# Layer norm statistics in two halves about a lower-half pivot, and the roots of three norms moved from GpSimd's power to ScalarE's Sqrt with VectorE's reciprocal, in a two-block transformer kernel

## The chip, the cores and the metric

The kernel runs on one core of one Trainium2 chip. The metric is device time in microseconds (us), the median of several executions. A core has five engines that matter here: TensorE (PE; its weight loads are PEld), VectorE (DVE), ScalarE (ACT), GpSimd (POOL) and SyncE (SP, which issues DMAs). They run their own instruction streams and wait for each other by semaphores.

## The reference, cut to what matters

256 tokens of width 1024 pass through two transformer blocks in float32. The first has a recurrent branch, sparse attention and a convolutional feed-forward part; its second norm is an RMS norm. The second has attention with a spatial gating unit and a gated feed-forward part; both of its sums are followed by a layer norm over all 1024 columns.

```python
def rms_norm(x, g):
    x32 = x.astype(jnp.float32)
    y = x32 * lax.rsqrt(jnp.mean(x32 * x32, axis=-1, keepdims=True) + EPS)
    return (y * g.astype(jnp.float32)).astype(x.dtype)
...
def layer_norm(x, g, b):
    xf = x.astype(jnp.float32)
    mu = jnp.mean(xf, axis=-1, keepdims=True)
    var = jnp.mean(jnp.square(xf - mu), axis=-1, keepdims=True)
    return ((xf - mu) * lax.rsqrt(var + LN_EPS) * g.astype(jnp.float32) + b.astype(jnp.float32)).astype(x.dtype)
...
        x = layer_norm(DEEPNORM_ALPHA * x + mix, ln1_g[l], ln1_b[l])
        ffn = swiglu_ffn(x, w_gate[l], w_up[l], w_down[l])
        x = layer_norm(DEEPNORM_ALPHA * x + ffn, ln2_g[l], ln2_b[l])
```

## The kernel before

The 256 tokens are two tiles of 128, one token per partition, called tile 0 and tile 1 (`t`). All weights come from HBM as one stream of chunks (`CHUNKS`), mostly 128x2048 float32. For each chunk ScalarE writes a rounded high part (`split`, L614, into `WH`), VectorE the remainder (L1033, into `WL`), and TensorE multiplies high by high, low by high and high by low. Activations are kept in the same two parts (`BHL`, `CHL`, `AH`, `AL`). The program of each engine is one loop over the chunks, written out by hand: what an engine does for chunk `c` stands in `side(c)`, in that order, and nothing is reordered later.

Three places hold the norms that the change touches. A norm needs whole rows, so it lies between two stages of matmuls:

- **The RMS norm before the feed-forward part of block one** (chunk kind "wo"). VectorE adds the residual (L1298), ScalarE squares each half of 512 columns with a running sum (L809), VectorE joins the two sums (L1303), GpSimd raises the result to the power -0.5 (L576), VectorE scales (L1310), TensorE transposes (L1754), ScalarE and VectorE write the high and low parts of the transposed tile (L918, L1443).
- **Layer norm one** (chunk kind "wo2", `layer_norm(0)`), between the second block's output projection and the gated feed-forward part.
- **Layer norm two** (`layer_norm(1)`), after the last matmul; its halves go to the output by DMA (L535). This is the end of the program.

In a layer norm VectorE forms the residual sum of a half (`residual_sum`, L1515) with the row's sum in `ysum`, then the negative mean (`mean`, L1541). Then two things run side by side: ScalarE squares all 1024 columns about the mean (`norm_squares`, L930), and VectorE forms (y + (-mean)) * gain (`gain`, L1526). GpSimd turns the sum of squares into 1/sqrt(var + eps) in two instructions (`power`, L554 and L555), and VectorE finishes each half with * yrs + bias (`finish`, L1535). In VectorE's program `residual_sum` of tile 1's first half stands ahead of `finish` of tile 0.

`link(...)` marks an instruction whose engine waits for its own result before it goes on. In row 85.37 us below, L554 is another use of `power`, for the keys of block one.

Of the kernel before, what the change touches and what calls it, by code (L numbers as in the profile page):

```python
# [27 lines left out]
P = 128  # L28
TOK = 256
NT = TOK // P  # L30
DM = 1024
# [204 lines left out]
def two_block_program(nc, A_w, A_x, A_cols, A_consts, A_g1, A_g2, A_og, A_gln, A_ln1, A_ln2, A_ws, A_out):  # L236
    ctx = ExitStack()
    with ctx:
# [30 lines left out]
        IDR = put("IDR", [P, P], F32R)  # L269
# [15 lines left out]
        def const(name):  # L285
# [5 lines left out]
        half = small("half", 64)  # L291
# [36 lines left out]
        yss = small("yss", 4)  # L328
        yrs = small("yrs", 4)
        tmp = small("tmp", 80)  # L330
# [98 lines left out]
        m_hi, m_lo, x1_ready, x1_sq, x1_ss, x1_rstd, xn2_ready, xt2_done, xt2_hi = (sem(n) for n in (  # L429
            "m_hi", "m_lo", "x1_ready", "x1_sq", "x1_ss", "x1_rstd", "xn2_ready", "xt2_done", "xt2_hi"))  # L430
# [10 lines left out]
        y_mean, y_sq, y_rstd, y_ln, xt4_done, xt4_hi, xt4_lo, up2_silu, up2_prod = (sem(n) for n in (  # L441
            "y_mean", "y_sq", "y_rstd", "y_ln", "xt4_done", "xt4_hi", "xt4_lo", "up2_silu", "up2_prod"))
        up2_hi, up2_lo, z_gain, masks_ready, wt_ready, rnn_in, xw_ready, gate_t_done, x_sq2 = (sem(n) for n in (
            "up2_hi", "up2_lo", "z_gain", "masks_ready", "wt_ready", "rnn_in", "xw_ready", "gate_t_done", "x_sq2"))
        half_copied, halves_summed = sem("half_copied"), sem("halves_summed")

# [93 lines left out]
        def _(eng):  # L540
# [57 lines left out]
        def _(eng):  # L598
# [123 lines left out]
            def side(c):  # L722
# [82 lines left out]
                if kind == "wo" and i % 2:  # L805
                    for t in range(NT):
                        n = i // 2
                        eng.wait_ge(x1_ready, NT * n + t + 1)
                        eng.activation(JK[:, 2 * n + t, :], X1[:, t, 512 * n:512 * n + 512], ACT.Square, scale=DM ** -0.5,  # L809
                                       accum_out=ss1[:, 2 * t + n:2 * t + n + 1]).then_inc(x1_sq, 1)  # L810
# [1622 lines left out]
```

## Time and profile before

| | |
|---|---|
| median of 3 executions | 824.15 us (824.13 to 825.29) |
| the profiled execution: its own time | 824.04 us |
| the profiled execution: span from first to last instruction | 822.3 us |
| mean granted TensorE clock | 0.993 |
| PE busy | 808.8 us (98%) |
| VectorE busy | 588.0 us (72%) |
| ScalarE busy | 481.3 us (59%) |
| GpSimd busy | 31.3 us (4%) |

How to read it: an engine that is busy for 98% of the span sets the time nearly everywhere, so a change on the other engines can only matter where TensorE waits or has already ended. Times in rows are us from the span's start, and "idle before <-" names what ended an engine's idle time.

### The profile page before, as it was taken

The page shows a single profiled execution, that of the slowest core. Times are in us where ns is not written, and L with a number is a line of the kernel's source. Part 1 is how long each engine was busy: PE and PEld are TensorE (multiplying, and loading weights), DVE is VectorE, ACT ScalarE, POOL GpSimd, SP SyncE. Part 2 cuts the span into 40 slices and gives each one's busy share as a digit, 9 for nine tenths or more (in the row PEclk, how much of TensorE's full clock was granted, in tenths as well). Part 3 has the DMA queues.
Part 4 walks back from the last instruction along what each step waited for, and adds up shares of the span by engine and source line. Part 5 has one row for each costly group of instructions (what it writes and reads, how often), then busy time and mean ns, then how long its engine had stood idle before and what let it go on. Part 6 is the DMA issues. An engine that isn't in the chain of part 4 may idle for free.

```text
span 822.3 us, 12246 instructions
## 1 busy us (share of the span) xinstructions
PE 808.8 (98%) x4997; PEld 706.5 (86%) x4997; DVE 588.0 (72%) x751; ACT 481.3 (59%) x730; POOL 31.3 (4%) x46
## 2 busy tenths in 40 slices
PE   9999998999999999999999999999999999999996
PEld 8889896888898998988888888888788988888885
DVE  5684686898975775788677877877877655654655
ACT  6463676878666444667566656546665645544551
POOL 1103000000000000000000000020110000000000
PEclk9999998999999999999999999999999999999998
DMA  8436441514234675255545555574344554565441
GB/s 327 157 123 268 151 168 50 169 55 164 100 121 173 221 272 206 103 188 194 200 185 199 166 204 200 211 271 158 132 179 151 205 205 168 191 209 200 157 151 51
DMA packets 22631, 144.00 MB, mean 175 GB/s; under 512 B 2608, under 2 KB 3120, under 8 KB 8240
## 3 DMA queue, kind: packets, MB, share of 16 engines
q1 hardware_dynamic: 20880, 137.92, 47.2%
q10 hardware_dynamic: 1696, 5.31, 1.8%
q8 instruction: 39, 0.64, 0.3%
q14 instruction: 16, 0.13, 0.0%
HBM read 142.17 MB, written 1.05 MB: 174 GB/s over the span
## 4 chain that ended last, share of the span: by engine, by line
PE 91%; DVE 3%; ACT 3%; issue 1%; DMA 1%; POOL 0%; DVEq 0%; POOLq 0%; SPq 0%; ACTq 0%
PE PS L1678 19%; PE PS L1682 10%; PE PS L1731 9%; PE PS L1732 9%; PE PS L1735 9%; PE PS L1665 7%; PE PS L1666 6%; PE PS L1670 6%; PE PS L1825 2%; PE PS L1694 2%; PE PS L1791 1%; PE PS L1802 1%; PE PS L1995 1%; PE PS L1702 1%; PE PS L2003 1%
## 5 line engine op out<-in xcount | busy, mean ns | idle before, releaser
L1033 DVE TENSOR_TENSOR WL<-RAW,WH 128x2048 fp32r<-128x2048 f32 (+2 forms) x128 | 285.1, 2228 | 45.9 <-ACT WH L614 45.9
L614 ACT ACTIVATE WH<-RAW 128x2048 fp32r<-128x2048 f32 (+2 forms) x128 | 238.7, 1867 | 67.7 <-PE PS L1735 26.5
L1453 DVE TENSOR_TENSOR HLS<-PS,HLS 128x512 f32<-128x512 f32 x46 | 31.7, 689 | 92.8 <-ACT HLS L938 92.8
L1678 PE MATMUL PS<-CHL,WH 128*128 128x512 f32 x352 | 87.9, 392 | 0.0
L1665 PE MATMUL PS<-BHL,WH 128*126 128x256 f32 (+2 forms) x344 | 85.7, 287 | 0.4 <-ACT TI L788 0.4
L1666 PE MATMUL PS<-BHL,WH 128*126 128x256 f32 (+2 forms) x344 | 83.6, 282 | 0.0
L938 ACT ACTIVATE HLS<-PS 128x512 f32<-128x512 f32 x46 | 27.4, 595 | 90.8 <-PE PS L1682 86.4
L1678 PE MATMUL PS<-BHL,WH 128*128 128x512 f32 x320 | 79.9, 392 | 0.0
L1678 PEld LDWEIGHTS PS<-CHL,WH 128*128 128x128 f32 x352 | 63.9, 189 | 11.8
L1732 PE MATMUL PS<-WH,AL 128*128 128x512 f32 x176 | 68.8, 391 | 0.0
L1665 PEld LDWEIGHTS PS<-BHL,WH 128*126 128x126 f32 (+2 forms) x344 | 64.3, 187 | 5.2 <-issue 4.3
L1731 PE MATMUL PS<-WH,AH 128*128 128x512 f32 x176 | 68.7, 390 | 0.0
L1678 PEld LDWEIGHTS PS<-BHL,WH 128*128 128x128 f32 x320 | 58.1, 189 | 10.7
L1666 PEld LDWEIGHTS PS<-BHL,WH 128*126 128x126 f32 (+2 forms) x344 | 64.4, 187 | 0.0
L1731 PE MATMUL PS<-WH,BHL 128*128 128x512 f32 x160 | 63.2, 395 | 0.0
L1732 PE MATMUL PS<-WH,BHL 128*128 128x512 f32 x160 | 62.4, 390 | 0.0
L1735 PE MATMUL PS<-WL,AH 128*128 128x512 f32 x176 | 54.4, 390 | 0.0
L1682 PEld LDWEIGHTS PS<-CHL,WL 128*128 128x128 f32 x352 | 48.0, 190 | 3.4
L1682 PE MATMUL PS<-CHL,WL 128*128 128x256 f32 x352 | 49.1, 282 | 0.0
L1670 PE MATMUL PS<-BHL,WL 128*126 128x256 f32 (+2 forms) x344 | 47.7, 281 | 0.0
L1682 PEld LDWEIGHTS PS<-BHL,WL 128*128 128x128 f32 x320 | 43.6, 190 | 3.1
L1464 DVE SCALAR_TENSOR_TENSOR CG<-HLS,CV,CG 128x255 f32<-128x255 f32 (+1 forms) x96 | 44.1, 480 | 1.7
(312 smaller groups left out, 1379.2 us busy)
## 6 DMA issues: line engine op xcount, KB each, us to landing
RAW<-in_w_stream SPq DMA_DIRECT2D x108, 1024.0 KB, 4.8
RAW<-in_w_stream SPq DMA_DIRECT2D x11, 1008.0 KB, 4.9
RAW<-in_w_stream SPq DMA_DIRECT2D x8, 704.0 KB, 4.5
WF<-in_w_stream SPq DMA_DIRECT2D x2, 1024.0 KB, 4.7
LN<-in_ln ACTq DMA_DIRECT2D x2, 1024.0 KB, 5.4
WF<-in_w_stream SPq DMA_DIRECT2D x4, 294.0 KB, 2.9
X<-in_x SPq DMA_DIRECT2D x2, 512.0 KB, 4.2
RAW<-in_w_stream SPq DMA_DIRECT2D x2, 512.0 KB, 7.3
```

The source lines that it names most:

```text
L614: eng.activation(WH[:, c % NSLOT, 0:CHUNKS[c][2]], raw(c), ACT.Copy).then_inc(w_hi, 1)
L1033: eng.tensor_tensor(WL[:, c % NSLOT, 0:CHUNKS[c][2]], raw(c), f32(WH[:, c % NSLOT, 0:CHUNKS[c][2]]), ALU.subtract).then_inc(w_lo, 1)
L1453: eng.tensor_tensor(HLS[:, n % 4, :, :], PS[:, bank:bank + 2, 0:TOK], HLS[:, n % 4, :, :], ALU.add)\
L1464: ins = eng.scalar_tensor_tensor(o, HLS[:, i % 4, v, 0:TOK - s], col("fw", (2 - s) * 2 * N_UP + f), o, ALU.mult, ALU.add)
L1665: eng.matmul(out, wh, H[0:parts, k, :], start=(k == 0), stop=False)
L1666: eng.matmul(out, wh, L[0:parts, k, :], start=False, stop=False)
L1670: last = eng.matmul(out, wl, H[0:parts, k, :], start=False, stop=(k == nk - 1))
L1678: eng.matmul(PS[:, bank, :], wh, HL[:, k, :, :].rearrange("p a t -> p (a t)"), start=(k == 0), stop=False)
L1682: last = eng.matmul(PS[:, bank, 0:TOK], wl, HL[:, k, 0, :], start=False, stop=(k == KD - 1))
L1731: eng.matmul(out, H[:, k, tile], wh, start=(start and n == 0), stop=False)
L1732: eng.matmul(out, L[:, k, tile], wh, start=False, stop=False)
L1735: last = eng.matmul(out, H[:, k, tile], WL[:, s, lo_:lo_ + cols], start=False, stop=(stop and n == len(ks) - 1))
```

## The change

It has five parts.

1. A layer norm's squares are no longer taken about the mean of 1024 columns but about a pivot, the mean of the tile's lower 512 columns (`ypiv`, one new VectorE instruction behind the first residual sum). ScalarE squares the lower half as soon as the pivot is there (`norm_first`) and the upper half when its residual sum is there (`norm_root`). With S0 and S1 the two halves' sums, the variance is (all squares about the pivot) / 1024 - ((S0 - S1) / 1024)^2. GpSimd works out `yadd`, which is the lower half's part of it plus eps minus the correction, in four linked instructions, in place of two before.
2. ScalarE takes the root: Sqrt(upper squares / 1024 + `yadd`), and VectorE a reciprocal (`root`), in place of GpSimd's power. The RMS norm of block one gets the same: its pair of sums is joined inside ScalarE's Sqrt, and GpSimd has no part in it.
3. In a layer norm, `gain` is cut into halves, and `finish` of tile 0 stands ahead of `residual_sum` of tile 1's first half. For tile 1 of layer norm one each half's finish follows its own gain.
4. `root_table()` runs a one-column Sqrt on ScalarE ahead of each place, which brings Sqrt's table in. The built program has four table loads more than before: three of these, and one for Gelu at the second chunk of block one's feed-forward part.
5. `IDR`, a rounded copy of the identity matrix that nothing read, goes, with TensorE's wait for it.

```diff
@@ gpsimd
-            for t in range(NT):
-                eng.wait_ge(x1_ss, t + 1)
-                eng.tensor_tensor(rs1[:, t:t + 1], ss1s[:, t:t + 1], half[:, 0:1], ALU.pow).then_inc(x1_rstd, 1)
...
-            for n in range(2):
-                for t in range(NT):
-                    eng.wait_ge(y_sq, NT * n + t + 1)
-                    j = NT * n + t
-                    power(yrs[:, j:j + 1], yss[:, j:j + 1], 1, DM, LN_EPS, y_rstd)
+            for j in range(2 * NT):
+                d, add, s = ydif[:, j:j + 1], yadd[:, j:j + 1], 2 * j
+                eng.wait_ge(y_first, j + 1)
+                link(eng.tensor_scalar(add, ysqa[:, j:j + 1], 1.0 / DM, LN_EPS, ALU.mult, ALU.add))
+                eng.wait_ge(y_half, j + 1)
+                link(eng.tensor_scalar(d, ysum[:, s:s + 1], ysum[:, s + 1:s + 2], 1.0 / DM, ALU.subtract, ALU.mult))
+                link(eng.tensor_tensor(d, d, d, ALU.mult))
+                eng.tensor_tensor(add, add, d, ALU.subtract).then_inc(y_add, 1)
@@ scalar
                         if i == 3:
+                            link(squares)
+                            eng.wait_ge(x1_ss, t + 1)
+                            eng.activation(std1[:, t:t + 1], ss1[:, 2 * t + 1:2 * t + 2], ACT.Sqrt,
+                                           bias=ss1s[:, t:t + 1]).then_inc(std_ready, 1)
...
-            def norm_squares(n, t):
+            def norm_first(n, t):
 
                 j = NT * n + t
-                eng.wait_ge(y_mean, j + 1)
-                eng.activation(YJ[:, t, :], (X1 if n == 0 else X3)[:, t, :], ACT.Square, bias=ymean[:, j:j + 1],
-                               accum_out=yss[:, j:j + 1]).then_inc(y_sq, 1)
+                eng.wait_ge(y_pivot, j + 1)
+                eng.activation(YJ[:, t, 0:512], (X1 if n == 0 else X3)[:, t, 0:512], ACT.Square, bias=ypiv[:, j:j + 1],
+                               accum_out=ysqa[:, j:j + 1]).then_inc(y_first, 1)
+
+            def norm_root(n, t):
+
+                j = NT * n + t
+                eng.wait_ge(y_half, j + 1)
+                link(eng.activation(YJ[:, t, 512:DM], (X1 if n == 0 else X3)[:, t, 512:DM], ACT.Square,
+                                    bias=ypiv[:, j:j + 1], accum_out=ysqb[:, j:j + 1]))
+                eng.wait_ge(y_add, j + 1)
+                eng.activation(ystd[:, j:j + 1], ysqb[:, j:j + 1], ACT.Sqrt, bias=yadd[:, j:j + 1], scale=1.0 / DM)\
+                   .then_inc(std_ready, 1)
+
+            def root_table():
+
+                eng.activation(junk[:, :], ident[:, 0:1], ACT.Sqrt)
@@ vector, residual_sum
-                link(eng.scalar_tensor_tensor(o, o, ALPHA, PS[:, 2 * t + h, :], ALU.mult, ALU.add,
-                                              accum_out=ysum[:, k:k + 1]))
+                ins = eng.scalar_tensor_tensor(o, o, ALPHA, PS[:, 2 * t + h, :], ALU.mult, ALU.add,
+                                               accum_out=ysum[:, k:k + 1])
+                if h:
+                    ins.then_inc(y_half, 1)
+                    eng.wait_ge(y_half, j + 1)
+                else:
+                    link(ins)
+                    eng.tensor_scalar(ypiv[:, j:j + 1], ysum[:, k:k + 1], -2.0 / DM, None, ALU.mult).then_inc(y_pivot, 1)
@@ vector, layer_norm
+                def root(t):
                     j = NT * n + t
-                    eng.wait_ge(y_rstd, j + 1)
-                    eng.wait_ge(y_gain, j + 1)
...
+                    eng.wait_ge(std_ready, NT + j + 1)
+                    link(eng.reciprocal(yrs[:, j:j + 1], ystd[:, j:j + 1]))
```

**Where instructions move.** VectorE at the end of the program, layer norm two, before (`X_158` is the tile being normed, `X_134` the gained copy):

```order
L1515 SCALAR_TENSOR_TENSOR X_158,ysum<-X_158,PS 128x512 x2
L1541 TENSOR_SCALAR ymean<-ysum 128x1
L1526 SCALAR_TENSOR_TENSOR X_134<-X_158,ymean,LN_159 128x1024
L1515 SCALAR_TENSOR_TENSOR X_158,ysum<-X_158,PS 128x512
L1535 SCALAR_TENSOR_TENSOR X_158<-X_134,yrs,LN_159 128x512
L1515 SCALAR_TENSOR_TENSOR X_158,ysum<-X_158,PS 128x512
L1541 TENSOR_SCALAR ymean<-ysum 128x1
L1526 SCALAR_TENSOR_TENSOR X_134<-X_158,ymean,LN_159 128x1024
L1535 SCALAR_TENSOR_TENSOR X_158<-X_134,yrs,LN_159 128x512 x3
```

and in the changed kernel, the same place, up to tile 1's mean (its gains, reciprocal and finishes follow as for tile 0):

```order
L1551 SCALAR_TENSOR_TENSOR X_164,ysum<-X_164,PS 128x512
L1558 TENSOR_SCALAR ypiv<-ysum 128x1
L1551 SCALAR_TENSOR_TENSOR X_164,ysum<-X_164,PS 128x512
L1586 TENSOR_SCALAR ymean<-ysum 128x1
L1568 SCALAR_TENSOR_TENSOR X_140<-X_164,ymean,LN_165 128x512 x2
L1574 RECIPROCAL yrs<-ystd 128x1
L1580 SCALAR_TENSOR_TENSOR X_164<-X_140,yrs,LN_165 128x512 x2
L1551 SCALAR_TENSOR_TENSOR X_164,ysum<-X_164,PS 128x512
L1558 TENSOR_SCALAR ypiv<-ysum 128x1
L1551 SCALAR_TENSOR_TENSOR X_164,ysum<-X_164,PS 128x512
```

Both of tile 0's finishes now precede tile 1's first residual sum; before, one stood between tile 1's two sums and the other behind tile 1's gain.

VectorE in layer norm one, tile 1, from the low parts of tile 0 (`BHL`) on, before:

```order
L1443 TENSOR_TENSOR BHL<-PS,BHL 128x2x128 x4
L1515 SCALAR_TENSOR_TENSOR X_134,ysum<-X_134,PS 128x512
L1541 TENSOR_SCALAR ymean<-ysum 128x1
L1526 SCALAR_TENSOR_TENSOR X_158<-X_134,ymean,LN_153 128x1024
L1535 SCALAR_TENSOR_TENSOR X_158<-X_158,yrs,LN_153 128x512 x2
```

and now, from the two instructions that have come in ahead of these low parts:

```order
L1551 SCALAR_TENSOR_TENSOR X_140,ysum<-X_140,PS 128x512
L1558 TENSOR_SCALAR ypiv<-ysum 128x1
L1478 TENSOR_TENSOR BHL<-PS,BHL 128x2x128 x4
L1551 SCALAR_TENSOR_TENSOR X_140,ysum<-X_140,PS 128x512
L1586 TENSOR_SCALAR ymean<-ysum 128x1
L1568 SCALAR_TENSOR_TENSOR X_164<-X_140,ymean,LN_159 128x512
L1574 RECIPROCAL yrs<-ystd 128x1
L1580 SCALAR_TENSOR_TENSOR X_164<-X_164,yrs,LN_159 128x512
L1568 SCALAR_TENSOR_TENSOR X_164<-X_140,ymean,LN_159 128x512
L1580 SCALAR_TENSOR_TENSOR X_164<-X_164,yrs,LN_159 128x512
```

The second half's gain has moved behind the first half's finish.

## Rows read from the trace of the kernel before

**Rows 1.** The page, part 4: the chain that ended last, by engine.

```profile
PE 91%; DVE 3%; ACT 3%; issue 1%; DMA 1%; POOL 0%; DVEq 0%; POOLq 0%; SPq 0%; ACTq 0%
```

**Rows 2.** TensorE's waits: total us, times, longest us.

```profile
PE PS L1754 <- DVE X L1535: 0.6, 1, 0.6
```

**Rows 3.** Timeline of VectorE, 806 to 823 us: start, duration, instruction, [idle before].

```profile
810.09 0.69 DVE L1515 SCALAR_TENSOR_TENSOR X<-X,PS 128x512 f32<-128x512 f32 x1
...
811.14 1.28 DVE L1526 SCALAR_TENSOR_TENSOR X<-X,ymean,LN 128x1024 f32<-128x1024 f32 x1
813.43 0.69 DVE L1515 SCALAR_TENSOR_TENSOR X<-X,PS 128x512 f32<-128x512 f32 x1 [1.00 <-PE PS L1735]
...
814.84 0.68 DVE L1515 SCALAR_TENSOR_TENSOR X<-X,PS 128x512 f32<-128x512 f32 x1
...
815.56 0.21 DVE L1541 TENSOR_SCALAR ymean<-ysum 128x1 f32<-128x1 f32 x1
815.81 1.28 DVE L1526 SCALAR_TENSOR_TENSOR X<-X,ymean,LN 128x1024 f32<-128x1024 f32 x1
817.01 0.75 DVE L1535 SCALAR_TENSOR_TENSOR X<-X,yrs,LN 128x512 f32<-128x512 f32 x1
818.47 1.42 DVE L1535 SCALAR_TENSOR_TENSOR X<-X,yrs,LN 128x512 f32<-128x512 f32 x2 [0.71 <-POOL yrs L555]
```

**Rows 4.** Timeline of ScalarE, 806 to 823 us.

```profile
815.81 1.15 ACT L930 ACTIVATE YJ<-X,ymean 128x1024 f32<-128x1024 f32 x1 [3.50 <-DVE ymean L1541]
```

**Rows 5.** Timeline of GpSimd, 806 to 823 us.

```profile
812.39 0.19 POOL L554 TENSOR_SCALAR tmp<-yss 128x1 f32<-128x1 f32 x1 [179.66 <-ACT YJ L930]
...
817.13 0.67 POOL L554 TENSOR_SCALAR tmp<-yss 128x1 f32<-128x1 f32 x1 [3.93 <-ACT YJ L930]
817.89 0.54 POOL L555 TENSOR_TENSOR yrs<-tmp,half 128x1 f32<-128x1 f32 x1
```

**Rows 6.** Timeline of GpSimd, two more instructions, elsewhere.

```profile
85.37 1.11 POOL L554 TENSOR_SCALAR tmp<-css 64x1 f32<-64x1 f32 x1 [11.14 <-ACT KSQ L665]
...
608.38 0.90 POOL L555 TENSOR_TENSOR ors<-tmp,half 128x1 f32<-128x1 f32 x1
```

**Rows 7.** Timeline of VectorE at these two times.

```profile
84.14 2.29 DVE L1033 TENSOR_TENSOR WL<-RAW,WH 128x2048 fp32r<-128x2048 f32 x1 [4.86 <-ACT WH L614]
...
608.12 0.75 DVE L1435 SCALAR_TENSOR_TENSOR MR<-MR,ors,OGR 128x512 f32<-128x512 f32 x1 [1.16 <-POOL ors L555]
```

**Rows 8.** Groups of instructions: count, busy us, mean ns, idle before.

```profile
L965 ACT ACT_TABLE_LOAD x1 | 1.3, 1283 | 0.0
L744 ACT ACTIVATE l<-l 126x11 f32<-126x11 f32 x1 | 0.2, 212 | 0.0
...
L1408 DVE RECIPROCAL ri<-rs 128x16 f32<-128x16 f32 x1 | 0.3, 254 | 0.1
...
L930 ACT ACTIVATE YJ<-X,ymean 128x1024 f32<-128x1024 f32 x4 | 4.6, 1153 | 17.8 <-DVE ymean L1541 17.8
```

**Rows 9.** Timeline of ScalarE at the RMS norm of block one.

```profile
318.14 0.63 ACT L809 ACTIVATE JK<-X 128x512 f32<-128x512 f32 x1 [2.96 <-DVE X L1298]
```

**Rows 10.** Timeline of VectorE, layer norm one.

```profile
624.02 1.29 DVE L1526 SCALAR_TENSOR_TENSOR X<-X,ymean,LN 128x1024 f32<-128x1024 f32 x1
...
626.33 1.42 DVE L1535 SCALAR_TENSOR_TENSOR X<-X,yrs,LN 128x512 f32<-128x512 f32 x2
628.28 1.42 DVE L1443 TENSOR_TENSOR BHL<-PS,BHL 128x256 fp32r<-128x256 f32 x4 [0.53 <-ACT BHL L918]
...
630.58 1.28 DVE L1526 SCALAR_TENSOR_TENSOR X<-X,ymean,LN 128x1024 f32<-128x1024 f32 x1
632.77 1.41 DVE L1535 SCALAR_TENSOR_TENSOR X<-X,yrs,LN 128x512 f32<-128x512 f32 x2 [0.90 <-POOL yrs L555]
```

**Rows 11.** Timeline of TensorE: tile 1's transposes at the two inner norms.

```profile
334.06 1.18 PE L1754 MATMUL PS<-CN,XN 128*128 128x128 f32 x8
...
633.57 1.32 PE L1754 MATMUL PS<-CN,X 128*128 128x128 f32 x8 [0.56 <-DVE X L1535]
```

More of the change, by code:

```diff
@@ L288, in two_block_program @@
         ident = const("ident")
-        half = small("half", 64)
+        half = small("half", 16)
         ssx = small("ssx", 4)
@@ L872, in side @@
                     evict_hi(CH, XT_BANKS["m"], mrt_done, mrt_hi, kps=(0, 1), first=2)
+                if kind == "wo2" and i == 0:
+                    root_table()
+                    norm_first(0, 0)
                 if kind == "wo2" and i == 2:
-                    norm_squares(0, 0)
+                    norm_root(0, 0)
                     split(c + 2)
@@ L997, in _ @@
                     eng.wait_ge(const_in, 32)
-                    eng.activation(IDR[:, :], ident, ACT.Copy).then_inc(masks_ready, 1)
                 if rg_group(c - W0, RG_INPUT) == NG - 1:
@@ L1521, in layer_norm, with gain, finish @@
                 gains, gains_in, landed = ((LN1, rows_in, 48), (LN2, rows_in, 64))[n]
[L1523 removed]
+                def gain(t, h):
                     j = NT * n + t
[L1525 to L1526 removed]
+                    half = slice(512 * h, 512 * h + 512)
+                    eng.scalar_tensor_tensor(gained[:, t, half], y[:, t, half], ymean[:, j:j + 1], gains[:, 0, half],
                                              ALU.add, ALU.mult).then_inc(y_gain, 1)
[L1529 removed]
+                def root(t):
                     j = NT * n + t
[L1531 to L1536 removed]
+                    eng.wait_ge(std_ready, NT + j + 1)
+                    link(eng.reciprocal(yrs[:, j:j + 1], ystd[:, j:j + 1]))
+                def finish(t, h):
+                    j = NT * n + t
+                    half = slice(512 * h, 512 * h + 512)
+                    eng.wait_ge(y_gain, 2 * j + h + 1)
+                    eng.scalar_tensor_tensor(X3[:, t, half], gained[:, t, half], yrs[:, j:j + 1], gains[:, 1, half],
+                                             ALU.mult, ALU.add).then_inc(y_ln, 1)
                 def mean(t):
@@ L1540, in mean @@
                     k = 4 * n + 2 * t
[L1541 to L1542 removed]
+                    link(eng.tensor_scalar(ymean[:, j:j + 1], ysum[:, k:k + 1], ysum[:, k + 1:k + 2], -1.0 / DM, ALU.add, ALU.mult))
                 if n == 0:
@@ L1547, in layer_norm @@
                     eng.wait_ge(gains_in, landed)
-                    gain(0)
+                    gain(0, 0)
+                    gain(0, 1)
+                    root(0)
+                    finish(0, 0)
+                    finish(0, 1)
                     residual_sum(0, 1, 0)
-                    finish(0)
                     tile_lo(BH, BL, XT_BANKS[4], xt4_hi, xt4_lo, 0)
@@ L1553, in layer_norm @@
                     mean(1)
-                    gain(1)
-                    finish(1)
+                    gain(1, 0)
+                    root(1)
+                    finish(1, 0)
+                    gain(1, 1)
+                    finish(1, 1)
                     tile_lo(BH, BL, XT1_BANKS[4], xt4_hi, xt4_lo, 1)
@@ L1561, in layer_norm @@
                     eng.wait_ge(gains_in, landed)
-                    gain(0)
+                    gain(0, 0)
+                    gain(0, 1)
+                    root(0)
+                    finish(0, 0)
+                    finish(0, 1)
                     residual_sum(1, 1, 0)
-                    finish(0, (0,))
                     residual_sum(1, 1, 1)
                     mean(1)
-                    gain(1)
-                    finish(0, (1,))
-                    finish(1)
+                    gain(1, 0)
+                    gain(1, 1)
+                    root(1)
+                    finish(1, 0)
+                    finish(1, 1)
             def gained_lo(kp):
```

70 lines of the change are left out of this document (38 added, 32 removed).

## The prediction

> **What bounds the kernel now.** I read the page's chain first: TensorE carries 91% of it [rows 1]. Then TensorE's waits, for the places where a norm holds it up. At the touched norms the only one of weight is 0.6 us, at layer norm one, where it waits for VectorE's finish [rows 2]. So the change can pay in two places: at layer norm one, up to that wait and what follows it, and behind the last matmul, where the norm's own chain is the time. The timelines of the tail show that chain: tile 1's last residual sum at 814.84, mean at 815.56, gain at 815.81 beside ScalarE's squares of 1.15 us, GpSimd's two instructions from 817.13 to 818.43, and two finishes from 818.47 to 819.89 [rows 3 to 5]. From there to the end of the span, 2.4 us, lies the last DMA, which the change leaves alone.
>
> **The tail, what is meant to go.** The long way from mean to finish is ScalarE 1.15 us, GpSimd 0.67, GpSimd 0.54, with hops. The squares of the lower half start earlier, and the power goes. But VectorE is then the engine with most to do: both finishes of tile 0 come ahead of tile 1's sums.
>
> **The tail, what comes in.** The four new GpSimd instructions fall beside VectorE's gains. The profile shows what happens there. GpSimd's one-column tensor_scalar takes 0.19 us when VectorE is quiet, but 0.67 when issued 0.12 us into a finish, and it ends at 817.80, just behind the finish's end at 817.01 + 0.75 = 817.76 [rows 3, 5]. The same form took 1.11 us at 85.37 and ended at 86.48, VectorE's L1033 beside it at 86.43; the power at 608.38 took 0.90 in place of 0.54 beside L1435 [rows 6, 7]. In all three VectorE reads two tensors from SBUF. The gain reads two as well. So I count a GpSimd instruction as held until VectorE's instruction ends, plus 0.05.
>
> The Trainium skill says this outright (SBUF — State Buffer, "Who interferes with whom"): a VectorE instruction with two SBUF inputs contends with a GpSimd instruction that reads SBUF, and the loser fully blocks, for the whole instruction. By that rule the tail gets slower, as in the sum below. The same page lets the first to start win; by that VectorE's gain would also wait for the first GpSimd instruction, at most its 0.19 us in each tile, which I leave out.
>
> Tile 0, step by step. The pivot takes the place of the second sum at 810.09. No row has this instruction; between nothing and the mean's 0.21 us [rows 3] I take 0.1, since only its issue holds VectorE. Second sum 810.19; from it to the gain were 1.05 us (810.09 to 811.14), so gain at 811.24. Two of 512 columns take 1.42 like the pair of finishes [rows 3]: to 812.66. ScalarE: pivot read at 810.3, then 0.63 us of squares of 512 columns [rows 9], and 0.17 to GpSimd's start as before (816.96 to 817.13) [rows 4, 5]: the first GpSimd instruction runs at 811.1 to 811.3, just ahead of the gain. The second is issued at 811.4 and held to 812.71. The third and fourth take 0.19 each with 0.09 between, as between 817.80 and 817.89 [rows 5]: 813.27. ScalarE's Sqrt costs 0.21, like the one small activation in the profile, and the reciprocal 0.25 [rows 8], with hops of 0.04 (818.43 to 818.47): finish at 813.85. For one column the reciprocal may be less, the Sqrt hardly; 0.1 us either way.
>
> Tile 1. Two finishes are passed in 1.34 (the pair's 1.42 less the second's overlap), so the first sum starts at 815.19. It stood at 813.43, before the finish. Pivot 0.72 later (814.84 to 815.56), second sum 816.01, mean 816.73, gains 816.98 to 818.40, second GpSimd instruction 818.45, fourth 819.01, Sqrt 819.26, reciprocal, finish 819.59. Before it was 818.47. **Tail: +1.1 us.** Without the hold the GpSimd chain would end before the gains: tile 0's finish 812.87, tile 1's sums 814.21 and 815.03, gains 816.0 to 817.34 (pitch), finish 817.63: -0.8 us. These are the bounds.
>
> **Layer norm one.** Tile 0's gain stays at 624.02. The third GpSimd instruction falls onto it and is held to 625.49; by the same steps the finish starts at 626.35, as before (626.33) [rows 10]. Then one sum and a pivot now follow these finishes where only a sum preceded them: VectorE was free at 627.75 (0.53 before 628.28), now it is at 628.5, and the low parts start 0.2 late. This passes on to tile 1's gain, 630.77. Only one half is gained: GpSimd is held to 631.57, fourth instruction 631.85, Sqrt 632.10, finish of the first half 632.43, against 632.77. But the second half's gain follows, and its finish waits for that gain: 633.90, against 632.77 + 0.67 = 633.44. TensorE transposes four blocks earlier and the last four 0.46 later than at 633.57 and on [rows 11]. Of this I take +0.3, since high and low parts of the four pieces ran in one row behind each other and hide some. Bounds: +0.5, and -0.2 without the hold, where both halves come 0.15 or more earlier. **+0.3 us.**
>
> **RMS norm of block one.** The power (0.54 us, as at 817.89 [rows 5]) and VectorE's join (one column, at most the mean's 0.21 [rows 3]) give way to Sqrt, 0.21, and reciprocal, 0.25 [rows 8], and one hop goes: 0.3 us less at most. But TensorE came to tile 1's transposes at 334.06 without idle before them [rows 11], so this is hidden. The cover is TensorE's own work on tile 0; without it the 0.3 would count. **0**, at best -0.1.
>
> **Four table loads** of 1.28 us [rows 8]. Ahead of the first squares of the RMS norm ScalarE idled 2.96 us [rows 9], and the four squares of the layer norms have 17.8 us of idle before them [rows 8], the first tile of each most of it: hidden. The one before Gelu follows ScalarE's copy, and TensorE has no wait in the feed-forward stage [rows 2]: hidden; bare it would cost 1.28. The dropped `IDR` frees ScalarE early, where nothing waits for it: 0.
>
> **Sum.** 822.3 + 1.1 + 0.3 = 823.7 us of span; the profiled execution lay 1.74 above its span and 0.11 under the median. **825.5 us.** A measurement of this kernel can tell about 0.2% (1.65 us) from no change, so this is no change that one can see.
>
> **Rivals.**
> - *GpSimd isn't held, or hardly* (one row of the same form, at 812.39, is clean; but VectorE had just gone quiet). -0.8 and -0.2 give 823.15. The new instructions would have to fall into gaps, and two gains stand back to back. 0.17.
> - *GpSimd slips in between the two gains.* No row shows a held instruction before a second VectorE instruction of that kind. One step of 0.28 less in each tile of the tail: 824.95. 0.17.
> - *The hold takes the first instruction too.* In the tail it is due 0.1 us from the gain in both tiles. If it misses, another 0.28 per tile in the tail, and 0.3 at layer norm one if its second is caught: 1.7 + 0.6 = +2.3 us, 826.4. This is the slower side: it decides once GpSimd's first instruction is issued after the gain. 0.14.
> - *A table load is bare* after all, for example at the end, if ScalarE's last high part comes late: at most 1.28 on top. 0.03.
> - *The forecast*: 0.49, its own range 825.0 to 826.0.
>
> The range of 823.1 to 826.1 leaves out most of the last two rivals. Faster by over 0.2% (under 822.5) needs more than the free case gives: 0.06. Slower (over 825.8) is the third rival, the fourth, and the upper edge of the forecast: 0.20. The rest, 0.74, is within 0.2%.
>
> **What would show it.** In the changed kernel's tail, GpSimd's second instruction in each tile should take over 1 us and end just behind the second gain; VectorE should idle 1.0 us or more before each reciprocal; the last finish should start near 819.6. At layer norm one the second half's transposes should wait about 0.5 us behind the first half's. I am wrong if GpSimd's four instructions take 0.19 each beside the gains, or if ScalarE's Sqrt takes much more than 0.21.

## The result, and the profile after

The changed kernel took 826.36 us (median of 17 executions, 823.95 to 828.42) beside 824.13 for the kernel before (17, 821.77 to 825.44). The ratio is 1.0029, with a 95% interval of 1.0020 to 1.0037: slower, by 2.2 us. The forecast was 825.5, with a range of 823.1 to 826.1; the time lies 0.26 above that range.

The page of the changed kernel, its head and part 1:

```profile
span 823.5 us, 12293 instructions
PE 807.4 (98%) x4997; PEld 705.9 (86%) x4997; DVE 590.2 (72%) x765; ACT 490.1 (60%) x750; POOL 32.9 (4%) x52
```

Where the 2.2 us are can't be read from two spans alone. The span grew by 1.2 in the profiled executions (822.3 to 823.5), but by 1.9 in the medians over all executions (822.2 to 824.1). And the time around the span, execution time less span, grew as well: 1.75 to 2.22 in the median.

The 0.7 us by which the profiled executions differ less is TensorE's clock, in a stage that the change doesn't touch. Here are four windows of the kernel before, columns as on the page's windows (length, busy time of each engine, PEclk, DMA share, GB/s):

```profile
130.00:132.00 2.00, 0.31 (x1) 0.31 (x2) 1.93 (x5) 1.36 (x3) 0.00 (x0) 0.90 0.87 359
132.00:134.00 2.00, 2.00 (x6) 1.08 (x7) 1.00 (x2) 0.00 (x0) 0.00 (x0) 0.50 0.24 101
134.00:136.00 2.00, 2.00 (x10) 0.84 (x7) 0.00 (x0) 0.34 (x1) 0.00 (x0) 0.50 0.00 0
136.00:138.00 2.00, 2.00 (x10) 1.26 (x11) 0.00 (x0) 2.00 (x5) 0.00 (x0) 0.50 0.00 0
```

and two of the same windows in the changed kernel:

```profile
134.00:136.00 2.00, 2.00 (x12) 0.92 (x8) 0.00 (x0) 0.51 (x2) 0.00 (x0) 0.71 0.00 0
136.00:138.00 2.00, 2.00 (x17) 1.17 (x16) 0.00 (x0) 2.00 (x4) 0.00 (x0) 1.00 0.00 0
```

Behind a stretch in which TensorE was nearly idle (busy 0.31 us of the first window's 2), its granted clock was 0.5, that is 1.2 GHz instead of 2.4, for 6.8 us in one execution and 3.4 in the other; in roots_only below not at all. Laid instruction by instruction against the kernel before, TensorE in the changed kernel comes out of this stage 1.51 us early and gives 0.77 back by 175 us, 0.43 of it in one wait for ScalarE at 161.8. What is left, 0.74, is luck of the execution, and has to be taken off before the rest is read. In such a comparison TensorE then falls behind at just two places: by 0.66 at 366.8 us and by 0.29 at 633.6; another 0.08 comes in small pieces between 586 and 629. Behind TensorE's work, the tail is longer by 0.88. Together 1.9, as in the median spans.

**The tail.** VectorE's timeline of the changed kernel, answering to [rows 3]:

```profile
809.65 0.69 DVE L1551 SCALAR_TENSOR_TENSOR X<-X,PS 128x512 f32<-128x512 f32 x1 [4.18 <-PE PS L2158]
...
811.42 1.44 DVE L1568 SCALAR_TENSOR_TENSOR X<-X,ymean,LN 128x512 f32<-128x512 f32 x2
813.61 0.17 DVE L1574 RECIPROCAL yrs<-ystd 128x1 f32<-128x1 f32 x1 [0.74 <-ACT ystd L961]
813.81 1.42 DVE L1580 SCALAR_TENSOR_TENSOR X<-X,yrs,LN 128x512 f32<-128x512 f32 x2
...
816.91 1.42 DVE L1568 SCALAR_TENSOR_TENSOR X<-X,ymean,LN 128x512 f32<-128x512 f32 x2
819.44 0.16 DVE L1574 RECIPROCAL yrs<-ystd 128x1 f32<-128x1 f32 x1 [1.12 <-ACT ystd L961]
819.64 1.42 DVE L1580 SCALAR_TENSOR_TENSOR X<-X,yrs,LN 128x512 f32<-128x512 f32 x2
```

From the first residual sum to the last pair of finishes it is 819.64 - 809.65 = 9.99 us; before it was 9.11, from the sum at 809.36, one 0.73 ahead of the first of [rows 3], to 818.47. GpSimd in the same stretch, answering to [rows 5]:

```profile
811.47 0.19 POOL L597 TENSOR_SCALAR yadd<-ysqa 128x1 f32<-128x1 f32 x1 [179.82 <-ACT YJ L951]
811.76 0.60 POOL L599 TENSOR_SCALAR ydif<-ysum 128x1 f32<-128x1 f32 x1
812.44 0.48 POOL L600 TENSOR_TENSOR ydif<-ydif 128x1 f32<-128x1 f32 x1
813.00 0.19 POOL L601 TENSOR_TENSOR yadd<-yadd,ydif 128x1 f32<-128x1 f32 x1
816.96 0.75 POOL L597 TENSOR_SCALAR yadd<-ysqa 128x1 f32<-128x1 f32 x1 [3.77 <-ACT YJ L951]
817.80 0.67 POOL L599 TENSOR_SCALAR ydif<-ysum 128x1 f32<-128x1 f32 x1
818.56 0.19 POOL L600 TENSOR_TENSOR ydif<-ydif 128x1 f32<-128x1 f32 x1
818.83 0.19 POOL L601 TENSOR_TENSOR yadd<-yadd,ydif 128x1 f32<-128x1 f32 x1
```

Where VectorE is quiet, three of the four take 0.19 each and the second 0.29 (gain_waits, below). In each tile two are held, and each ends 0.05 to 0.16 behind the end of one of the two gains: one goes through per gain, not one per pair. In tile 0 the second and third are held, and VectorE waits 0.74 for the root. In tile 1 it is the first and second, and it waits 1.12. The first is issued 0.05 us behind the start of the gain in both tiles, gets in in one and is held in the other; no run shows what decides that.

ScalarE, answering to [rows 4]: squares of 512 columns about a pivot, and a root:

```profile
810.57 0.72 ACT L951 ACTIVATE YJ<-X,ypiv 128x512 f32<-128x512 f32 x1 [6.01 <-DVE ypiv L1558]
...
819.11 0.29 ACT L961 ACTIVATE ystd<-ysqb,yadd 128x1 f32<-128x1 f32 x1 [1.54 <-POOL yadd L601]
```

**TensorE's waits**, two rows of that view of the changed kernel. The first answers to [rows 2], the second is new:

```profile
PE PS L1809 <- DVE X L1580: 0.8, 1, 0.8
PE PS L1790 <- DVE WL L1067: 0.6, 1, 0.6
```

**Gelu's table load.** ScalarE's, VectorE's and TensorE's timelines of the changed kernel, a row or two each. The load goes ahead of the first Gelu:

```profile
343.80 1.28 ACT L988 ACT_TABLE_LOAD   x1
345.10 0.42 ACT L988 ACTIVATE CG<-CG 128x256 f32<-128x256 f32 x1
```

```profile
345.55 0.42 DVE L1506 TENSOR_TENSOR CG<-CG 128x256 f32<-128x256 f32 x1 [0.55 <-ACT CG L988]
```

```profile
366.76 0.73 PE L1790 MATMUL PS<-WL,AH 128*128 128x512 f32 x2 [0.63 <-DVE WL L1067]
```

VectorE waits 0.55 for the Gelu. 21 us and four chunks later TensorE waits 0.63 for a low part of the weights. In between, VectorE's rows repeat every 5.87 us (346.80, 352.67, 358.54 for the low part of a chunk) and hold no idle time but the 0.48 that each chunk has before L1511, so it can't catch up; TensorE needs 5.59 per chunk (its own rows repeat at 348.27, 353.86 and 359.45) and runs up to it.

**Layer norm one**, tile 1, answering to [rows 10, 11]; VectorE, then TensorE's transposes:

```profile
632.07 0.16 DVE L1574 RECIPROCAL yrs<-ystd 128x1 f32<-128x1 f32 x1 [0.74 <-ACT ystd L961]
632.27 0.75 DVE L1580 SCALAR_TENSOR_TENSOR X<-X,yrs,LN 128x512 f32<-128x512 f32 x1
632.93 0.75 DVE L1568 SCALAR_TENSOR_TENSOR X<-X,ymean,LN 128x512 f32<-128x512 f32 x1
633.72 0.75 DVE L1580 SCALAR_TENSOR_TENSOR X<-X,yrs,LN 128x512 f32<-128x512 f32 x1
```

```profile
633.07 0.66 PE L1809 MATMUL PS<-CN,X 128*128 128x128 f32 x4
634.52 0.66 PE L1809 MATMUL PS<-CN,X 128*128 128x128 f32 x4 [0.79 <-DVE X L1580]
...
635.89 1.31 PE L1749 MATMUL PS<-BHL,WH 128*128 128x256 f32 x8 [0.21 <-DVE BHL L1478]
```

The first half of the transposes comes 0.5 early and the second waits 0.79 behind it. TensorE then waits 0.21 more for low parts, and has lost 0.29 by the end of the norm.

### The profile page after: what moved, and what is told of

It reads as the page before. It is cut to its first block, busy times and chain, and to the rows that moved or that the text cites. A ratio compares the mean times of both kernels' runs of the same rounds, so it can differ in the third digit from the quotient of the medians.

```text
span 823.5 us, 12293 instructions
## 1 busy us (share of the span) xinstructions
PE 807.4 (98%) x4997; PEld 705.9 (86%) x4997; DVE 590.2 (72%) x765; ACT 490.1 (60%) x750; POOL 32.9 (4%) x52
## 4 chain that ended last, share of the span: by engine, by line
PE 63%; issue 24%; DVE 6%; ACT 5%; DMA 1%; POOL 1%; DVEq 0%; SPq 0%; POOLq 0%; ACTq 0%
PE PS L1733 8%; PE PS L1790 7%; PE PS L1786 7%; PE PS L1787 7%; PE PS L1720 6%; PE PS L1721 6%; PE PS L1725 6%; PE PS L1737 4%; DVE WL L1067 2%; PE PS L1879 1%; PE PS L2049 1%; PE PS L1856 1%; PE PS L1845 1%; PE PS L1749 1%; ACT SM L642 1%
```

## The experiments

Eleven kernels, each compared with the kernel before on its own chip. "Around" is the median of execution time less span; "tail" runs from the first residual sum of layer norm two to its last pair of finishes in the profiled execution.

| kernel | median us (n) | before | ratio, 95% interval | around | tail |
|---|---|---|---|---|---|
| before | 823.98 (35) | | | 1.75 | 9.11 |
| changed | 826.36 (17) | 824.13 | 1.0029 (1.0020 to 1.0037) | 2.22 | 9.99 |
| gelu_early | 825.39 (12) | 823.98 | 1.0017 (1.0007 to 1.0027) | 2.24 | 9.64 |
| rms_power | 825.28 (11) | 823.98 | 1.0016 (1.0007 to 1.0024) | 1.74 | 9.99 |
| add_vector | 824.84 (12) | 823.98 | 1.0014 (1.0005 to 1.0023) | 1.75 | 9.04 |
| roots_only | 822.92 (12) | 823.98 | 0.9989 (0.9979 to 0.9999) | 1.72 | 8.70 |
| pool_probe | 824.13 (10) | 824.00 | 1.0001 (0.9990 to 1.0012) | 1.73 | 9.11 |
| load_only | 824.67 (11) | 824.00 | 1.0010 (0.9998 to 1.0021) | 1.73 | 9.11 |
| roots_order | 823.09 (11) | 824.00 | 0.9991 (0.9982 to 1.0000) | 1.78 | 8.34 |
| gain_waits | 826.86 (5) | 824.00 | 1.0037 (1.0024 to 1.0050) | 2.23 | 10.50 |
| pool_two_more | 825.36 (10) | 823.97 | 1.0014 (1.0003 to 1.0025) | 1.72 | 9.64 |
| vector_two_more | 825.63 (10) | 823.97 | 1.0020 (1.0012 to 1.0029) | 2.23 | 9.97 |
| roots_all | 823.12 (12) | 823.97 | 0.9983 (0.9973 to 0.9992) | 1.75 | 8.71 |

**gelu_early.** The changed kernel, with Gelu's table fetched behind the RMS norm's last root instead of at the first Gelu.

```diff
                             eng.activation(std1[:, t:t + 1], ...).then_inc(std_ready, 1)
+                            if t == NT - 1:
+                                eng.activation(junk[:, :], ident[:, 0:1], ACT.Gelu_apprx_tanh)
```

> The changed kernel with one more instruction: a one-column Gelu on ScalarE behind the Sqrt of tile 1 of the RMS norm, so that Gelu's table comes in at about 332 us, in an idle stretch of 1.9 us. Theory (the load in the feed-forward stage is bare, because ScalarE and VectorE together need 5.87 us per chunk there against TensorE's 5.59 and can't make up for it): TensorE's wait of 0.63 us for VectorE's low part at 366.8 goes, VectorE's idle of 0.55 before L1506 at 345.5 too, and the time falls by 0.6 us, from about 826.4 to 825.8. Rival (that wait has to do with TensorE having come early by the clock's shorter low stretch, not with the load): the wait stays and the time stays at 826.4.

The wait for `WL` was gone, and no offset of TensorE arose in the feed-forward stage. ScalarE loaded the table at 331.04 us, in idle time. The median was 1.0 us below the changed kernel's, with 0.6 expected: 0.65 for the load, and 0.35 because in its tail the first GpSimd instruction slipped in ahead of the hold in both tiles (VectorE waited 0.74 twice) and not in one. The time around the span stayed at 2.24.

**load_only.** The other side of it: the kernel before, with one Sqrt ahead of the RMS norm's squares and nothing else. It brings in two loads, Sqrt's there and Gelu's at 344 us.

```diff
                 if kind == "wo" and i % 2:
+                    if i == 1:
+                        eng.activation(junk[:, :], ident[:, 0:1], ACT.Sqrt)
```

> The kernel before plus the dummy Sqrt ahead of the RMS norm alone: two table loads more (Sqrt's in idle time, Gelu's in the feed-forward stage), nothing else. Theory: TensorE waits 0.6 us for a low part of the weights at about 367 us, and the time rises by 0.6 us to about 824.7. Rival (the wait needs something else of the change): no wait, 824.1.

Its view of TensorE's waits has the row again:

```profile
PE PS L1738 <- DVE WL L1036: 0.6, 1, 0.6
```

TensorE fell back by 0.65 at that place and nowhere else. The median rose by 0.67; its interval alone just reaches to no change, and the trace decides. vector_two_more, below, shows why medians alone would not do.

**rms_power.** The changed kernel with the RMS norm as it was: GpSimd's power, no Sqrt and so no load for it nor for Gelu.

```diff
+                eng.wait_ge(x1_ss, t + 1)
+                eng.tensor_tensor(rs1[:, t:t + 1], ss1s[:, t:t + 1], half[:, 0:1], ALU.pow).then_inc(std_ready, 1)
...
-                            eng.activation(std1[:, t:t + 1], ss1[:, 2 * t + 1:2 * t + 2], ACT.Sqrt,
-                                           bias=ss1s[:, t:t + 1]).then_inc(std_ready, 1)
```

> The changed kernel with block one's RMS norm as before (VectorE's join, GpSimd's power, no table load for Sqrt there and none for Gelu after it). Theory: everything that this part costs is the load before Gelu, so the time falls by 0.6 us to about 825.8, as with the early Gelu. Rival (the part's 0.3 us shorter norm pays in TensorE's stream): it falls by 0.3 or less, 826.1.

No wait in the feed-forward stage, as in gelu_early. The root itself is worth nothing there in either form. The median fell by 1.1 and not by the 0.6 expected: the time around the span was 1.74, a surprise, and that is the other 0.5. At layer norm one TensorE fell back by 0.59 in the profiled execution, twice as much as in the changed kernel, because ScalarE's Sqrt of tile 1 started 0.37 us behind GpSimd's last instruction and not 0.09; why it did is open. The tail was as long as the changed kernel's, with the tiles' parts exchanged: here it was tile 0 whose first GpSimd instruction was held:

```profile
811.16 0.75 POOL L600 TENSOR_SCALAR yadd<-ysqa 128x1 f32<-128x1 f32 x1 [180.10 <-ACT YJ L947]
...
816.99 0.19 POOL L600 TENSOR_SCALAR yadd<-ysqa 128x1 f32<-128x1 f32 x1 [3.76 <-ACT YJ L947]
```

**add_vector.** The changed kernel with `yadd` worked out on VectorE, in four one-column instructions more, and none on GpSimd.

```diff
+                    eng.tensor_scalar(ydif[:, j:j + 1], ysum[:, k:k + 1], ysum[:, k + 1:k + 2], 1.0 / DM, ALU.subtract, ALU.mult)
+                    eng.tensor_scalar(ydig[:, j:j + 1], ysum[:, k:k + 1], ysum[:, k + 1:k + 2], -1.0 / DM, ALU.subtract, ALU.mult)
...
+                    link(eng.tensor_scalar(ydif[:, j:j + 1], ydif[:, j:j + 1], ydig[:, j:j + 1], LN_EPS, ALU.mult, ALU.add))
+                    eng.wait_ge(y_first, j + 1)
+                    eng.scalar_tensor_tensor(yadd[:, j:j + 1], ysqa[:, j:j + 1], 1.0 / DM, ydif[:, j:j + 1], ALU.mult, ALU.add)\
+                       .then_inc(y_add, 1)
```

> The changed kernel with GpSimd's four one-column instructions gone; VectorE does the same arithmetic in four small instructions around the mean. Theory (GpSimd is held behind VectorE's gains): VectorE gets some 0.5 us more work per tile, but goes from gain to reciprocal without idle; tail's last finish 1.0 us earlier against its first sum than in the changed kernel (9.0 in place of 10.0 us), layer norm one 0.3 us earlier, time down by 1.3 us to about 825.1. Rival (the tail is long because VectorE has both finishes of tile 0 ahead of tile 1's sums): 0.5 us more work on VectorE per tile makes it longer, 0.5 to 1 us slower, about 827.

VectorE's timeline of this kernel, tile 1 of the tail:

```profile
817.77 1.41 DVE L1561 SCALAR_TENSOR_TENSOR X<-X,ymean,LN 128x512 f32<-128x512 f32 x2
819.10 0.16 DVE L1567 RECIPROCAL yrs<-ystd 128x1 f32<-128x1 f32 x1
819.29 1.41 DVE L1573 SCALAR_TENSOR_TENSOR X<-X,yrs,LN 128x512 f32<-128x512 f32 x2
```

No wait before the reciprocal. The tail is 9.04: the four instructions more delay each tile's gains by 0.57 us, and the whole is still 0.95 shorter than with GpSimd. At layer norm one TensorE falls back by 0.03 in place of 0.29. This shows that GpSimd's being late is what the changed tail pays for. It also shows that the two halves hardly gain anything even then: the tail is 0.07 below that of the kernel before, with VectorE busy nearly throughout it.

**gain_waits.** The hold tested by itself: VectorE's gains wait until GpSimd has finished, so nothing lies beside its four instructions.

```diff
+                    eng.wait_ge(y_add, j + 1)
```

> The changed kernel, in which VectorE's gains also wait until GpSimd's four instructions are through, so that none of them meets a gain. Theory (hold): GpSimd's take 0.19 each with 0.09 between, 0.9 us from the half's sum to the gain; the two gains then hide the Sqrt, and sum to finish takes 2.4 us per tile in place of 2.7 to 3.0: the tail gets 0.5 us shorter although VectorE is made to idle, time 825.9. At layer norm one, with one gain to hide behind, about nothing. Rival (no hold, GpSimd slow by itself): every instruction keeps its 0.5 to 0.7, the wait comes on top, and the tail gets 0.6 us longer per tile, 827.5.

GpSimd and VectorE in tile 1 of the tail of this kernel:

```profile
816.65 0.19 POOL L597 TENSOR_SCALAR yadd<-ysqa 128x1 f32<-128x1 f32 x1 [4.81 <-ACT YJ L951]
816.93 0.29 POOL L599 TENSOR_SCALAR ydif<-ysum 128x1 f32<-128x1 f32 x1
817.31 0.19 POOL L600 TENSOR_TENSOR ydif<-ydif 128x1 f32<-128x1 f32 x1
817.58 0.19 POOL L601 TENSOR_TENSOR yadd<-yadd,ydif 128x1 f32<-128x1 f32 x1
```

```profile
817.88 1.42 DVE L1569 SCALAR_TENSOR_TENSOR X<-X,ymean,LN 128x512 f32<-128x512 f32 x2 [1.32 <-POOL yadd L601]
```

The durations are those of a quiet VectorE: an instruction that was held for 0.48 to 0.75 us takes 0.19 when the gain is away, and the second, held for 0.60 to 0.67, takes 0.29. That decides for the hold. The time doesn't: the median of five executions lies 0.9 above the theory's and 0.6 below the rival's, and it went up, not down. From mean to finish it is 819.40 - 816.35 = 3.05 us, with 2.4 reckoned. The chain of four begins 0.30 us behind the start of the mean, since ScalarE's squares take 0.72, and costs 1.12; only then do the gains begin.

**pool_probe.** The hold measured on its own. The kernel before, with 60 pairs of a one-column tensor_scalar and a one-column memset on GpSimd, which nobody waits for, in the feed-forward stage of block one.

```diff
+            for _ in range(60):
+                link(eng.tensor_scalar(probe[:, 0:1], probe[:, 0:1], 1.0, 0.0, ALU.mult, ALU.add))
+                link(eng.memset(probe[:, 1:2], 0.0))
```

> The kernel before, with 120 extra GpSimd instructions on a scratch tile of its own, each linked to the one before: 60 times a one-column tensor_scalar (reads and writes SBUF) and a one-column memset (only writes), from about 333 us on, beside VectorE's work of the feed-forward stage. Theory (a GpSimd instruction that reads SBUF is held by a VectorE instruction with two SBUF inputs until that one ends, and slips in before the next): tensor_scalars take 0.19 us when VectorE is idle or reads PSUM (L1453), and up to 2.3 us beside L1033, ending 0.05 behind its end; beside the row of four L1464 they end one at each instruction's end, not behind the fourth. Memsets take about 0.1 to 0.2 everywhere. VectorE's own durations stay as they are (2.28, 0.48 each). Rival (first come, the whole engine held): tensor_scalars that have started hold VectorE, whose durations grow by up to 0.19. Time as before, 824.1. For the time outside the span: the program gets longer than the changed kernel's; if that time hangs on the program's total size, it rises from 1.75 to 2.2 us, otherwise it stays at 1.75.

GpSimd's timeline of this kernel, then VectorE's:

```profile
340.15 0.19 POOL L581 TENSOR_SCALAR probe<-probe 128x1 f32<-128x1 f32 x1
340.40 0.10 POOL L582 MEMSET probe<- 128x1 f32 x1
340.58 1.96 POOL L581 TENSOR_SCALAR probe<-probe 128x1 f32<-128x1 f32 x1
...
343.69 0.28 POOL L581 TENSOR_SCALAR probe<-probe 128x1 f32<-128x1 f32 x1
```

```profile
340.21 2.28 DVE L1039 TENSOR_TENSOR WL<-RAW,WH 128x2048 fp32r<-128x2048 f32 x1
342.40 1.91 DVE L1470 SCALAR_TENSOR_TENSOR CG<-HLS,CV,CG 128x255 f32<-128x255 f32 x4
```

Beside the one long instruction the tensor_scalar takes 1.96 us and ends at 342.54, 0.05 behind the 342.49 of VectorE. Beside the row of four short ones it takes 0.19 to 0.28: where one is held, it ends 0.05 behind the VectorE instruction that it started beside (the last one shown at 343.97, the third of the four at 343.92). The memset took 0.10 throughout. VectorE's durations stayed as they were (2283 ns for L1039, 480 for L1470), and the time did not change.

The Trainium skill (SBUF — State Buffer, "Who interferes with whom") says that a VectorE instruction with two SBUF inputs contends with a GpSimd instruction that reads SBUF, and that whoever issues first blocks the other for its whole instruction. For GpSimd as the second the trace agrees: 1.96 in place of 0.19 us. What the runs add is that the hold is one instruction long and not a row of them. For VectorE as the second the trace doesn't agree: GpSimd's tensor_scalar of 340.15 was under way when L1039 began at 340.21, and L1039 took 2.28 as in the kernel before.

**roots_only.** The kernel before with part 2 of the change for the layer norms alone: squares about the mean as they were, then ScalarE's Sqrt and VectorE's reciprocal; order, gain and RMS norm unchanged.

```diff
@@ scalar, norm_squares
+                eng.wait_ge(y_sq, j + 1)
+                eng.activation(ystd[:, j:j + 1], yss[:, j:j + 1], ACT.Sqrt, bias=lneps[:, 0:1], scale=1.0 / DM)\
+                   .then_inc(y_rstd, 1)
@@ vector, finish
-                    eng.wait_ge(y_rstd, j + 1)
+                    if 0 in halves:
+                        eng.wait_ge(y_rstd, j + 1)
+                        link(eng.reciprocal(yrs[:, j:j + 1], ystd[:, j:j + 1]))
```

> The kernel before with one part of the change alone: in the two layer norms ScalarE's Sqrt and VectorE's reciprocal in place of GpSimd's two instructions; squares about the mean, order of VectorE and RMS norm as before, Sqrt's table loaded ahead of the two places. Theory: the tail loses GpSimd's 0.67 + 0.54 and hops and gains 0.29 + 0.2, so the last finish starts at 817.9 in place of 818.5; layer norm one saves 0.2; time 0.6 to 0.8 us under before, 823.4. Rival (Sqrt with its load costs as much as the power): 824.1, no difference. If the time outside the span, which went from 1.74 to about 2.2 us with the change, hangs on the table loads or on Sqrt, it shows here too: then 823.9.

This one is faster than both kernels, than the one before by 0.11% (0.01 to 0.21). At layer norm one TensorE comes to tile 0's transposes 0.18 late, but its wait of [rows 2] is gone, and it comes out of the norm 0.37 earlier; the tail is 0.41 shorter. That is 0.8 us in the trace, the upper end of what was expected, and 1.1 in the medians. VectorE, tile 1 of the tail of this kernel:

```profile
813.48 1.28 DVE L1535 SCALAR_TENSOR_TENSOR X<-X,ymean,LN 128x1024 f32<-128x1024 f32 x1
814.68 0.74 DVE L1546 SCALAR_TENSOR_TENSOR X<-X,yrs,LN 128x512 f32<-128x512 f32 x1
815.35 0.15 DVE L1542 RECIPROCAL yrs<-ystd 128x1 f32<-128x1 f32 x1
815.53 1.41 DVE L1546 SCALAR_TENSOR_TENSOR X<-X,yrs,LN 128x512 f32<-128x512 f32 x2
```

There is no wait left before the reciprocal: the late half of tile 0's finish at 814.68 is what the root now waits for.

**roots_order.** roots_only with tile 0's finish in one piece ahead of tile 1's sums, as in the changed kernel.

```diff
+                    finish(0)
...
-                    finish(0, (0,))
...
-                    finish(0, (1,))
```

> The kernel with roots by ScalarE alone (squares about the mean), now with part three's order in layer norm two: both finishes of tile 0 ahead of tile 1's sums. Theory (with the root ready early, the order fills VectorE's idle second and takes a finish out of tile 1's chain): last finish 0.3 us earlier against the tail's first sum, 7.7 in place of 8.0 us; time 0.3 under roots alone, 822.6. Rival (the order as such is what makes the changed kernel's tail long, since tile 1's first sum comes 0.8 later): 0.5 us slower than roots alone, 823.4.

In the trace the tail is 8.34, 0.36 shorter than roots_only's: tile 1's gain starts 6.54 us behind the first sum in place of 6.65, and its finish 1.80 behind the gain in place of 2.05. The rest of the program is alike. So with the root ready early the order is no cost, and rather a gain; in the changed kernel it was not tested by itself. The medians don't show it (823.09 and 822.92, each with an interval of about 0.8 us either way), and which of the two is faster stays open.

**roots_all.** roots_only with the RMS norm's root on ScalarE as well, and the early load of Gelu's table.

```diff
+                            link(squares)
+                            eng.wait_ge(x1_ss, t + 1)
+                            eng.activation(std1[:, t:t + 1], ss1[:, 2 * t + 1:2 * t + 2], ACT.Sqrt,
+                                           bias=ss1s[:, t:t + 1]).then_inc(x1_rstd, 1)
+                            if t == NT - 1:
+                                eng.activation(junk[:, :], ident[:, 0:1], ACT.Gelu_apprx_tanh)
```

> Roots alone, as in roots_only, for both layer norms, with the RMS norm's root by ScalarE and VectorE's reciprocal too, and the Gelu table fetched early. Theory (the RMS norm's root is hidden behind TensorE's work on tile 0): no difference to roots_only, 822.9 us beside a kernel before at 824.0. Rival (some of it is on the path): 0.3 less, 822.6. If its time outside the span is 2.2 and not 1.7, the median is 0.5 higher, 823.4.

823.12, tail 8.71, and TensorE passes the RMS norm without an offset: the root there is hidden.

**pool_two_more and vector_two_more.** By then the time around the span was 2.2 in three kernels (changed, gelu_early, gain_waits) and 1.7 to 1.8 in all others, one with 120 more instructions among them. The three have the same numbers of GpSimd and VectorE instructions (52 and 765 on their pages). Both kernels here are the changed kernel with two memsets more at the start, of four columns each, one kernel on GpSimd and one on VectorE:

```diff
@@ gpsimd (pool_two_more)
+            link(eng.memset(ydif[:, :], 0.0))
+            link(eng.memset(yadd[:, :], 0.0))
@@ vector (vector_two_more)
+            link(eng.memset(ymean[:, :], 0.0))
+            link(eng.memset(yrs[:, :], 0.0))
```

> The changed kernel with two more one-column GpSimd memsets at the start of the program, where GpSimd is idle; nothing reads them. The time outside the span was 1.7 to 1.8 us in the kernel before and in five variants, and 2.2 in the changed kernel and in the two others that have the same numbers of GpSimd and VectorE instructions. Theory (the 0.48 us hang on how many instructions stand in an engine's program, or on where its last ones come to lie): with two more on GpSimd, time outside the span falls to 1.75 and the median to 825.9. Rival (they hang on something else that the changed kernel does): it stays at 2.2, and the median at 826.4.

> The changed kernel with two more one-column VectorE memsets at the start of the program; nothing reads what they write before it is written anew. Theory (number or place of instructions in VectorE's program): time outside the span falls to 1.75, median 825.9. Rival (GpSimd's program, or something else): it stays at 2.2, and the median at 826.4. If both kernels fall, the place of the whole program counts and not that of one engine; if neither does, the cause stays open.

With two more on GpSimd it fell to 1.72; with two more on VectorE it stayed at 2.23. Both kernels execute more than the changed one, so it isn't the work. It goes with GpSimd's program: 52 instructions on the page gave 2.2 in four kernels, and 36, 37, 39, 46, 54 and 167 gave 1.7 to 1.8 in the others. Of the rest of pool_two_more's 1.0 us, 0.35 is again the tail, where the first GpSimd instruction got in ahead in both tiles.

vector_two_more is also a warning. Its tail and its time around the span are those of the changed kernel, and yet its median, 825.63, is 0.73 below (826.4 was expected). Its executions had a higher mean clock more often: 0.996 or more in four of ten, against two of seventeen. That fits a difference of 0.7 us that the clock alone makes, and so the prices given here rest on the traces.

## Why the prediction was wrong

By its own steps, against the changed kernel:

- **"Four table loads … the one before Gelu follows ScalarE's copy, and TensorE has no wait in the feed-forward stage: hidden."** This is the step that failed. It cost 0.65 us (TensorE's loss at 366.8 us in the changed kernel and in load_only): the wait for `WL` appears in these two and in the others with the load at the Gelu, and not in gelu_early, rms_power or roots_all. That TensorE didn't wait in that stage said only that VectorE was no later than it. The view to read was VectorE's rhythm: no idle time in a chunk but the one after each Gelu, on a path that runs through ScalarE, so whatever delays the Gelu stays in the row. The price lay between the forecast's 0 and its bare 1.28. The rival that named it had 0.03.
- **"The profiled execution lay 1.74 above its span", taken as unchanged.** It became 2.22, 0.48 more. Two GpSimd memsets take it away again, so it comes with how GpSimd's program happens to lie or to be counted. No row shows it. What of the program sets it stays open.
- **The tail, +1.1.** Measured +0.88. GpSimd is held by the gains, as forecast (gain_waits, pool_probe, add_vector). Two sizes were off. The hold lasts one VectorE instruction, so one of GpSimd's slips in between the two gains, which was the rival of 824.95. That takes off what the rival said, 0.28 per tile: with neither first instruction caught the tail is +0.53 (gelu_early, pool_two_more), where 1.1 less 0.56 was the rival's figure. And the first instruction is sometimes caught too, the rival of 826.4, in one tile of two here; that adds 0.35 (+0.87 to +0.88 with one caught). The two partly cancel, and the forecast came out near by luck, for a reason it did not name. The rival's condition was wrong as well: the first instruction was issued behind the gain's start in all ten tiles of the five kernels with this code, and in seven of them it got in. ScalarE's root took 0.29 where 0.21 was reckoned, its squares 0.72 where 0.63, and the reciprocal 0.16 where 0.25.
- **The signs that the prediction named** came out in part: GpSimd's second instruction took 0.60 and 0.67 and not over 1 us, VectorE idled 0.74 and 1.12 before the reciprocals, and the last finish started at 819.64 as forecast, but from a first sum 0.29 later. And one of the prediction's rows doesn't bear its rule of "plus 0.05": the power at 608.38 ended at 609.28, 0.41 behind L1435's end at 608.87.
- **Layer norm one, +0.3.** Measured +0.29, and the mechanism as forecast: the first half early, the second waiting behind it, for 0.79 where about 0.5 was forecast. In tile 0 the hold was again one instruction long each time, and its finish came at 625.94 where 626.35 was reckoned.
- **RMS norm, 0.** Right: roots_all against roots_only.
- **The other three loads and `IDR`, 0.** Right: no offset of TensorE of 0.1 us or more at any other place, and ScalarE has its roots' table when it needs it.

The sum with the measured sizes: 0.88 + 0.29 + 0.65 + 0.48 = 2.3 us, against 2.2 in the medians. The forecast had 1.4. Of the missing 0.9, the table load is 0.65 and the time around the span 0.48; the tail's error, 0.2, is on the other side. Either of the two alone, with the tail's error, would have left the time within the range; it took both.

Why the change doesn't pay: its good part is the root by ScalarE and VectorE, which alone is worth 0.8 us in the trace of roots_only. The halves about a pivot bring GpSimd four instructions at the moment when VectorE's gains hold it, and at layer norm one they put the second half's gain between the root and the last finish. Fetching the roots' table for the RMS norm, where the root was hidden, puts a load before Gelu.

## What to carry to other kernels

When a function is added on ScalarE, look at where the next function's table must be loaded again, not only at the new one's; ask of that place whether the engine that waits for ScalarE has any idle time per round, for "TensorE doesn't wait here" is no cover. Small GpSimd work that reads SBUF belongs in gaps of VectorE, or beside instructions short enough to slip in between. Lay two traces against each other instruction by instruction before the spans are compared: here 0.7 us of clock hid over a third of what the change cost within the span.

## What had not been expected of the hardware

- A GpSimd instruction that is held gets in at the change between two VectorE instructions of a row: 0.19 to 0.28 us beside four of 0.48, against 1.96 beside one of 2.28. A memset, which reads nothing, isn't held at all (0.10).
- Where GpSimd's first instruction got in 0.05 us behind the start of the gains, the pair of gains took 1.44 to 1.45 us; where it was held, 1.41 to 1.42. With nothing beside them (gain_waits) they took 1.42. So VectorE seems to pay about 0.03 when it loses; that is seen in five kernels, and not tested by itself.
- The time around the span moved by 0.5 us with two idle memsets on GpSimd (2.22 to 1.72).
- In one stage TensorE's clock is granted at 0.5 for 0, 3.4 or 6.8 us behind a near-idle stretch, as the traces of this study show. Each step is worth about 1.5 us: TensorE came out of it 1.51 earlier with 3.4 us than with 6.8, and about 3 earlier with none (roots_only). The kernel before also had executions with a mean clock of 0.998 and a span of 820.2, beside 0.993 and 822.3 in its profile, which fits a stretch that was missing. Others had 0.992 and 823.5; no trace shows where they lost it.
